# Expert outputs scattered by token on the way out, smaller tails, and half of the first attention's output projection moved forward

## The reference

```python
# layer 0 and 1 (first_block), ALPHA = 4 ** 0.25
h = layer_norm(ALPHA * h + mix, ln_g[i, 0], ln_b[i, 0])
ffn = hier_moe(h, ...)                    # 32 experts, D_EXPERT = 512, top 2 of one group of 8
h = layer_norm(ALPHA * h + ffn, ln_g[i, 1], ln_b[i, 1])
# layer 2 (second_block)
x = x + concat([att, lru_out]) @ w_out
y = hierarchical_moe(rmsnorm(x, ffn_norm), ...)    # 32 experts, D_EXPERT_2 = 256, top 2
return rmsnorm(x + y, final_norm)

# diff_attention, per head of 8 (two score maps m, head_dim 64, value width 128)
p = softmax(where(mask, s * scale, -inf))
a = p[:, :, 0] - lam * p[:, :, 1]
o = einsum('bhqk,bhkd->bhqd', a, v)
o = o * rsqrt(mean(square(o), -1) + 1e-5) * sub_g
return (o * (1 - lambda_init)) @ w_o
```

## Time and profile before

| | |
|---|---|
| median of 3 runs | 2256.73 us (2256.59 to 2259.34) |
| the profiled execution | 2260.55 us, of which the span is 2258.7 us |
| mean granted clock of TensorE | 0.947 of full speed |
| busy share of the span | PE 89%, PEld 48%, DVE 31%, ACT 15%, POOL 3% |
| moved by DMA | 624.71 MB, mean 277 GB/s |

### The profile page before, as it was taken

The page is one execution under the profiler, slowest core; times in us unless marked ns, Lnnn a source line. Parts: engine busy times, 40 slices in busy tenths (PEclk is TensorE's granted clock), DMA queues, the critical chain, the costliest instruction groups (busy, mean ns, idle before and its releaser), DMA issues.

```text
span 2258.7 us, 26007 instructions
## 1 busy us (share of the span) xinstructions
PE 2018.9 (89%) x9962; PEld 1091.9 (48%) x9962; DVE 696.9 (31%) x1601; ACT 339.4 (15%) x758; POOL 71.0 (3%) x97
## 2 busy tenths in 40 slices
PE   8999779999999995899999999995599899879772
PEld 4444446545554452756545554452564445544441
DVE  0166645211111112445211111112546225311114
ACT  1133321100000000111100000000133221111110
POOL 0000000000000001000000000001100001100001
PEclk9999879999999998899999999998798899889997
DMA  9911102999999998422999999999521011689995
GB/s 339 365 43 38 56 4 94 364 420 421 421 421 421 420 421 332 182 82 94 365 420 421 421 421 421 421 421 341 155 75 43 32 38 59 240 355 421 421 420 215
DMA packets 144273, 624.71 MB, mean 277 GB/s; under 512 B 13264, under 2 KB 52272, under 8 KB 82768
## 3 DMA queue, kind: packets, MB, share of 16 engines
q1 hardware_dynamic: 119344, 567.24, 62.7%
q0 software_dynamic: 9504, 31.42, 4.1%
q10 hardware_dynamic: 15360, 25.18, 3.0%
HBM read 574.50 MB, written 49.28 MB: 276 GB/s over the span
## 4 chain that ended last, share of the span: by engine, by line
PE 72%; DMA 16%; DVE 7%; ACT 2%; issue 2%; POOL 0%; SPq 0%; POOLq 0%; ACTq 0%; DVEq 0%
PE bank L762 16%; PE bank L789 9%; PE bank L747 9%; DMA ring<-in_moe_w_up_dram 8%; PE bank L539 7%; PE bank L648 6%; DMA ring<-in_w_up_dram 5%; PE bank L510 5%; PE bank L551 4%; PE bank L771 3%; PE bank L943 1%; DVE h L1190 1%; PE bank L904 1%; PE bank L738 1%; PE bank L604 1%
## 5 line engine op out<-in xcount | busy, mean ns | idle before, releaser
L762 PE MATMUL bank<-ring,work 128*64 128x512 f32 x2048 | 454.1, 593 | 5.3 <-DMA ring<-in_moe_w_up_dram 4.9
L1463 DVE TENSOR_TENSOR work<-work,bank 64x512 f32<-64x512 f32 (+1 forms) x96 | 87.1, 907 | 816.1 <-ACT work L1057 816.0
L789 PE MATMUL bank<-ring,work 128*64 128x512 f32 x1280 | 299.1, 605 | 3.6
L762 PEld LDWEIGHTS bank<-ring,work 128*64 128x64 f32 x2048 | 148.3, 137 | 299.1 <-issue 298.6
L747 PEld LDWEIGHTS bank<-work 128*128 128x128 f32 x2112 | 245.8, 191 | 57.3 <-issue 52.9
L747 PE MATMUL bank<-work 128*128 128x128 f32 x2112 | 271.1, 281 | 0.1
L539 PE MATMUL bank<-hT,ring 128*128 128x512 f32 x384 | 183.1, 614 | 0.7 <-ACT work L998 0.7
L789 PEld LDWEIGHTS bank<-ring,work 128*64 128x64 f32 x1280 | 83.7, 137 | 146.9 <-issue 129.6
L1061 ACT ACTIVATE work<-bank 128x512 f32<-128x512 f32 x96 | 57.4, 597 | 620.2 <-PE bank L789 610.8
L771 PE MATMUL bank<-ring,work 128*64 128x256 f32 x1024 | 117.0, 381 | 16.1 <-DMA ring<-in_w_up_dram 15.7
L1057 ACT ACTIVATE work<-bank 64x512 f32<-64x512 f32 (+1 forms) x96 | 49.8, 518 | 509.4 <-PE bank L762 399.9
(11 more groups left out here) (259 smaller groups left out, 1632.4 us busy)
## 6 DMA issues: line engine op xcount, KB each, us to landing
ring<-in_moe_w_gate_dram SPq DMA_DIRECT2D x128, 1024.0 KB, 17.3
ring<-in_moe_w_up_dram SPq DMA_DIRECT2D x128, 1024.0 KB, 19.2
ring<-in_moe_w_down_dram SPq DMA_DIRECT2D x128, 1024.0 KB, 17.3
ring<-in_w_gate_dram SPq DMA_DIRECT2D x32, 1024.0 KB, 20.8
ring<-in_w_up_dram SPq DMA_DIRECT2D x32, 1024.0 KB, 24.2
ring<-in_w_down_dram SPq DMA_DIRECT2D x32, 1024.0 KB, 23.1
y_rows<-work ACTq DMA_DIRECT2D x192, 128.0 KB, 6.8
x_rows<-zeros SPq DMA_DIRECT2D x1, 12800.0 KB, 54.3
```

What stands on the lines that cost most here:

```text
L762: mm = pe.matmul(GU[BLK * a:BLK * a + BLK, :], xT_[:, 4 * kk + k, :], v[:, k, :], start=(kk + k == 0), stop=(kk + k == 4))
L789: mm = pe.matmul(DN[BLK * n:BLK * n + BLK, :], hT_[:, 2 * kk + k, :], v[:, k, 512 * n:512 * n + 512], start=(kk + k == 0), stop=(2 * kk + ...
L1463: dve.tensor_tensor(dealt(hg[:, 0:F], F // P), as_dealt(sg[:, 0:F], F // P), as_dealt(GU[BLK:P, 0:F], F // P), ALU.mult).then_inc(b.hg, 1)
```

## The change

It has five parts.

1. **Expert outputs.** `ysb` now holds a pair of experts as 128 whole rows. POOL writes them with one indirect transfer per pair to `y_rows`, which has two rows per token; slots without a token have an index out of bounds and are left out. To know the token of each slot, POOL first scatters, with eight indirect transfers of 128 elements of 4 bytes, the row numbers (`token`) into `slot_token` in HBM and loads them back as a table of 32 by 64. PE turns the table ahead of expert 2 (in layer 2 ahead of expert 3), and DVE makes `y_row` of it.
2. **Tails.** SP loads each tile's rows with one plain transfer of 1 MB instead of POOL's two gathers. DVE's order is changed so that tile 0 is finished first; sums of squares move to ACT. `project_turned` goes tile by tile through the first two units (128 columns a matmul) and does the other two units with 512 columns at the end.
3. **First attention.** One `tensor_tensor_reduce` per map takes the place of mask, maximum and scaling. Heads 0 to 3 are normalized, turned and kept in steps 25 to 31; steps 32 to 39 multiply them with their half of the output weights (`project_heads`), DVE adds that into `h` (`add_heads`). After the attention only heads 4 to 7 are left.
4. **Row scatter of layer 2.** The indices for `x_rows` are worked out per tile (`rows_of`), and the transfers of a tile start when its own are known.
5. Semaphores are merged; rows for overflowing experts have a table of their own (`y_over`).

```diff
@@ PE, first attention
+            def project_heads(i):
+                tt, n = i // 2, i % 2
+                u = first["wo"] + 2 * n
+                if tt == 0:
+                    wait_unit(pe, u)
+                    pe.wait_ge(at.placed, 4)
+                    pe.wait_ge(at.rope, 15 + i)
+                else:
+                    pe.wait_ge(at.added, i - 1)
...
+                else:
+                    project_heads(st)
                 if pair >= 1:
                     scores(step - 8)
...
+                if 28 <= step < 32:
+                    turn_head(step - 28)
@@ PE, mixture
+                    if type(i) is int and s == (2 if l < 2 else 3):
+                        pe.wait_ge(slots_loaded, 16 * (l + 1))
+                        pe.transpose(CT[0:BLK, 192:192 + E], slot_tab, ident[0:E, 0:E]).then_inc(slots_turned, 1)
@@ ACT, mixture
-                    for n in range(2):
-                        act.dma_start(y_rows[bass.ts(block_row, BLK), 512 * n:512 * n + 512],
-                                      ysb[s][BLK * n:BLK * n + BLK, :]).then_inc(b.y_stored[s], 16)
+                    act.activation(ysb[s // 2][rows, 0:512], DN[0:BLK, :], ACT.Copy)
+                    act.activation(ysb[s // 2][rows, 512:D], DN[BLK:P, :], ACT.Copy).then_inc(b.ysb, 1)
@@ DVE, first attention, per map m
-                    link(dve.tensor_tensor(sc[:, P * qb:P * qb + P], sc[:, P * qb:P * qb + P], causal, ALU.add))
-                    link(dve.tensor_reduce(mx[:, m:m + 1], sc[:, 0:P * (qb + 1)], AX, ALU.max))
-                    dve.tensor_scalar(negmax[:, m:m + 1], mx[:, m:m + 1], -0.125, None, ALU.mult).then_inc(at.negmax, 1)
+                    dve.tensor_tensor_reduce(out=sc, in0=sc, in1=cmask[:, P * (3 - qb):4 * P], scale=1.0, scalar=3e38,
+                                             op0=ALU.add, op1=ALU.min,
+                                             accum_out=negmax[:, m:m + 1]).then_inc(at.negmax, 1)
...
+                if step >= 33:
+                    add_heads(step - 33)
@@ POOL, mixture
+                for tt in range(T):
+                    for k in range(2):
+                        pool.indirect_dma_start(
+                            out=slot_token[l], out_offset=bass.IndirectOffsetOnAxis(
+                                ap=idx[:, T * k + tt:T * k + tt + 1], axis=0),
+                            in_=token[:, T * k + tt:T * k + tt + 1], in_offset=None).then_inc(slots_dealt, 16)
...
+                pool.wait_ge(slots_known, l + 1)
+                for q in range(E // 2):
+                    if l == 2 and 4 <= q + 3 <= E // 2:
+                        load_rows(q + 3)
+                    pool.wait_ge(main.ysb, main.n0 + 2 * q + 2)
+                    pool.indirect_dma_start(
+                        out=y_rows, out_offset=bass.IndirectOffsetOnAxis(ap=y_row[:, q:q + 1], axis=0),
+                        in_=ysb[q % 2], in_offset=None, bounds_check=2 * S - 1, oob_is_err=False)\
+                        .then_inc(main.y_stored[q % 2], 16)
@@ SP, tail
+                sp.dma_start(ytile[tt], y_rows[2 * P * tt:2 * P * tt + 2 * P, :].rearrange("(p k) d -> p (k d)", k=2))\
+                    .then_inc(routing.gathered[tt], 16)
```

More of the change, by code:

```diff
@@ L340, in program @@
         ygat = [[wk(8192 + 2048 * i + 1024 * k, 1024) for k in range(2)] for i in range(T)]
+        ytile = [wk(8192 + 2048 * i, 2 * D) for i in range(T)]
         hn = wk(8192, 8192).rearrange("p (t d) -> p t d", t=T)[:, :, 0:D]
@@ L374, in program @@
         orstd = sm(452, 32).rearrange("p (t n) -> p t n", t=T)
-        rstd2 = sm(484, 4)
+        rstd2, eps6 = sm(484, 4), sm(488, 1)
+        token, later = sm(489, 8), sm(497, 1)
         ojunk = sb("ojunk", [P, P])[:, :]
@@ L496, in _ @@
             mixture(2)
+            sp.wait_ge(y_landed, 3)
+            for tt in range(T):
+                load_tile(tt)
             for tt in range(T):
@@ L505, in _ @@
         def _(pe):
-            def project_tokens(u, banks, half, th):
-                v = ring[u % UNITS][:, :].rearrange("p (k n) -> p k n", k=K)
-                for k in range(K):
-                    mm = pe.matmul(banks[:, 256 * th:256 * th + 256], v[:, k, 128 * half:128 * half + 128],
-                                   hT[:, k, 256 * th:256 * th + 256], start=(k == 0), stop=(k == K - 1))
-                if th == 1:
-                    mm.then_inc(units_used if half else half_unit, 1)
@@ L535, in project_t @@
+                for i in range(2, 4):
+                    wait_unit(pe, u0 + i)
+                    for half in range(2):
+                        project_t(u0 + i, bank[2 * i + half], half)
             def project_t(u, banks, half, ks=range(K)):
@@ L610, in permute, with turn_head @@
                 pe.matmul(bank[cc % 2][:, :], rope_p, raw[cc % 2], start=True, stop=True).then_inc(at.perm, 1)
+            def turn_head(hh):
+                pe.wait_ge(at.normal, hh + 1)
+                for tt in range(T):
+                    mm = pe.transpose(bank[6][:, P * tt:P * tt + P], o1[:, tt, P * hh:P * hh + P], ident)
+                mm.then_inc(at.turned, 1)
+            def project_heads(i):
[7 more added lines that the diff above has]
+                    pe.wait_ge(at.added, i - 1)
+                v = ring[u % UNITS][:, :].rearrange("p (k n) -> p k n", k=4)
+                for k in range(4):
+                    mm = pe.matmul(bank[n][:, :], o1[:, tt, P * k:P * k + P], v[:, k, :], start=(k == 0), stop=(k == 3))
+                mm.then_inc(at.part, 1)
             pe.wait_ge(at.v, 2 * T)
@@ L1231, in _ @@
             dve.memset(zeros[:, :], 0.0).then_inc(zero_ready, 1)
+            link(dve.memset(eps6, 1e-6))
+            dve.wait_ge(const_loaded, 16)
+            link(dve.tensor_reduce(later, tri, AX, ALU.add))
+            for tt in range(T):
+                for k in range(2):
+                    ins = dve.tensor_scalar(token[:, T * k + tt:T * k + tt + 1], later, -2.0,
+                                            float(2 * P * (tt + 1) + k - 1), ALU.mult, ALU.add)
+            link(ins)
             dve.wait_ge(par.lam, 64)
```

424 lines of the change are left out of this document (272 added, 152 removed).

## The result

The changed kernel takes 2207.68 us (median of 4 runs, 2203.96 to 2208.96) against 2256.66 us: a ratio of 0.978, 95% interval 0.9763 to 0.9797. Its profiled execution took 2207.31 us, of which the span is 2205.4. The forecast was 2202 us, range 2182 to 2226.

A forecast was written before the change was run, and what follows sets the result against it. PE and DMA both near their limit in the long mixtures, DMA in layer 2, a serial chain in the attention's last pair. Terms +8 - 3 - 9 - 3 - 17 - 25 - 5.5 = -54.5 gave 2206, by median 2202 us, range 2182 to 2226.

The forecast's parts named there:

- The sum of steps, 2206: Whole kernel: the stage terms add to -54.5 us against the profiled execution's 2260.55; chance 0.60, range 2194 to 2212.
- The 3.8 us that I took off for the median: Whole kernel: the old profiled execution was 3.8 us above the median, so 2206 became 2202 us.
- 67 us for eight steps: First attention, last pair: projection, scores, maxima, exponentials, combination and addition in series, 7.25 to 9.6 us per block.
- 9 for the clock: First attention and head: about half of eight projections at 1.2 GHz, 2 us lost each, and a cold head start: +9.
- the moved matmuls gain almost nothing (-1 us): First attention and head, clock aside: +2 + 26 - 5 - 23.7, as the new place isn't parallel to the chain.
- the shorter maximum gains nothing up to step 31: First attention up to step 31: PE is the bound, so the shorter mask and maximum gain nothing.
- Mixtures of layers 0 and 1: Fewer store bytes keep DMA from becoming the bound, -4.3 us; with 1 for small waits, -3 us each.
- Rival B: Skipped slots move bytes or cost descriptors: -15 in layer 2, nothing in the other mixtures, 2218 us; chance 0.12.
- rival C: Slot scatters do not overlap, table 120 us late in each of the first two mixtures: 2430 us; chance 0.05.
- if the DMA rate falls with the scattered writes: Sign, without a size, that the prediction is wrong.
- 8.5 + 36.8 + 3 + 27.5: Layer 0's tail: DVE's first tile, four PE tiles of 9.2, cold start, 64 instructions of 512 columns; 75.6 us against 82.2.
- the account of DMA time: Layer 2's mixture, DMA-bound: hole about 9 us, dealing 8, stores 10, less 2, so -25 us.

The follow-up runs named there:

- the trace with nothing dealt: Kernel before the change, with the eight transfers that deal layer 2's rows and the wait for them left out: 2241.75 us against 2256.53.
- seven like traces: Profiled executions of the changed kernel and six kernels made from it, all with the same first attention; step 32 begins at 257.5 to 261.1 us.
- the three kernels with 8.4, 4.2 and no MB: Changed kernel with empty slots written too, 2225.22 us; the changed kernel itself, 2207.68; changed kernel with every expert-output slot skipped, 2192.90.
- the other six traces: Profiled attention and tail experiments with layer 2's POOL queue and 4.2 MB of stores as in the changed kernel; layer 2 mixtures of 261.7 to 262.9 us.
- the two runs above: Changed kernel with layer 2's loads of pairs 2 and 3 ahead of the slot scatters, 2207.83 us; changed kernel without layer 2's slot scatters, 2206.16 us.
- the projection last: Changed kernel with the kept heads' projection moved to the end of its step, behind scores and values: 2175.41 us, ratio 0.9638 to before.
- the exponentials first: Kernel with the scores first, plus ACT's exponentials ahead of its copy of the group before in steps 32 to 39: 2174.61 us, ratio 0.9632 to before.
- the scores first: Changed kernel with the scores of a step computed ahead of the kept heads' projection in steps 32 to 39: 2188.62 us, ratio 0.9703 to before.

## Why the prediction was right, and where not

The time was 5.7 us above the forecast. The sum of steps, 2206, was right to 1.3 us against the profiled execution, because its two errors, +6 and +8, were met by 13 us more than forecast from tails, mixtures and the stages between. That they met is luck. The 3.8 us that I took off for the median had no counterpart: the profiled execution of the changed kernel is at its median.

**First attention: the mechanism was right, the price of the move was hidden in it.** The chain was worked out as 67 us for eight steps plus 9 for the clock; the eight took 337.85 - 261.05 = 76.8 us. The projections took 39.1 instead of 27.5, so the clock cost 11.6 where the forecast had 9, and five of eight projections were hit where it had half. Each of the five that took 5.3 to 6.5 us came after PE had stood 2.5 to 2.8 us for DVE's addition; the three of 3.7 us came after waits of at most 1.4 us. The other terms were each one or two us small: the stretch from the last step to the head 11.7 against 9.6, the head 61.1 against 59. Together 14 against 8. What failed is the sentence that the moved matmuls gain almost nothing (-1 us). As a sum for the whole of part 3, clock aside, it came near (14.1 - 11.6 = 2.5); but it credited the move with what the single reduction gives. Undone alone, the move costs 24 us. That the shorter maximum gains nothing up to step 31 is not refuted: with the reduction alone step 32 begins at 255.1, in the old first attention at 257.7 and, in the trace with nothing dealt, at 257.2, which is within the spread of seven like traces. The gain lies behind step 32.

**Mixtures of layers 0 and 1: right**, -3.6 and -4.3 against -3 each. Rival B (a skipped slot costs as much as a full one) is refuted by the three kernels with 8.4, 4.2 and no MB; rival C (scatters one behind another) by the windows, in which PE never waits. The sign "if the DMA rate falls with the scattered writes" did not come: with all rows scattered, 1960 to 2160 moved 421 GB/s, and before the change 2000 to 2200 moved 420. The rule of the Trainium skill that I weighed (DMA: Bandwidth & Descriptors, section Measured: under 64 KB the descriptors dominate) may hold for the transfers themselves. No run shows it in the time here, for taking eight scatters of 512 bytes away changed the median by 1.5 us, within its spread.

**Tails: the mechanism was right, with one link overlooked in layer 0 and too much caution in layer 1.** In layer 0 the first tile lands 11.0 us after the last matmul (forecast 13.5, before 15.5):

```profile
895.91 4.89 DMA work<-y_rows
900.83 1.29 DVE h L1267
...
913.49 9.67 PE bank L548 x64
...
924.28 7.41 PE bank L548 x64
```

That is the chain of the changed kernel in tail 0; a tile costs PE 7.41 + 0.45 + 0.61 us and the waits between, 8.54, where I had 9.2; the first one took 9.67, a cold start of 2.3 (forecast 3). PE begins to turn tile 0 at 909.42, 8.6 us after the landing, as forecast (8.5); but it begins to project 12.7 us after it, where turn and copy should have taken 1.6 more. ACT's queue explains the rest:

```profile
912.61 0.20 ACT L1051 ACTIVATE small<-small 128x1 f32<-128x1 f32 x1 [7.05 <-DVE small L1281]
912.84 1.08 ACT L1041 ACTIVATE hT<-bank 128x512 f32<-128x512 f32 x2
```

The copies of the turned tile 0 (L1041) stand behind the square root of tile 1 (L1051), which waits for DVE's variance of tile 1. It is the link of the first attention again, worth some 2.5 us here; no run opened it. The sum itself, 8.5 + 36.8 + 3 + 27.5, is 75.8 and not 75.6; measured were 75.4. In layer 1 the landing takes 11.5 us, PE's work then goes as forecast but for a cold start of 1.0 us instead of 3.

**Layer 2: the step that failed is the account of DMA time**, "the hole of about 9 us, some 8 us of dealing, 4.2 MB of stores = 10 us, less 2". The mixture took 264.3 us, where "near 255" was to be seen. The windows give its bytes: 108.4 MB before, 102.0 after, and 102.0 to 102.2 in the other six traces. The 6.3 MB are 15 us at 420 GB/s: 4.2 MB of stores, 10 us as forecast, and only 2.1 MB of dealing, 5 us and not 8. Of the eight dealing transfers the last four start on POOL from 1908.67 to 1912.50, about when expert 0 does (1910.5), so their rows still land in the mixture. What is left of the 15.7 to 18.3 us that the mixture lost is 1 to 3 us for the hole, where the forecast had 9 - 2 = 7. With nothing dealt it was 4. So the dealing was 3 us too dear and the hole 4 to 6; together they are the 8 us. This is an account from rates and not an experiment: these 2.1 MB of dealing fall in the first microseconds, when no weight load is due before 1914.90, and whether they cost their 5 us wasn't tried. The slot scatters and the wait of 4.28 us are out as causes, by the two runs above.

**Last tail**: -5.9 against -5.5.

## What to carry to other kernels

Before work is moved from a busy stage into the gaps of another, follow the in-order queue of every engine round one step: if the moved piece stands ahead of anything that the next link of the chain needs, also through another engine's queue, it lengthens the chain by its own time. Here the same move of eight projections cost 24 us with them at the head of their steps and gained 7 (by the medians) with them at the end.

When several edits share a stage, undo each alone: one of two that the stage's time had netted was worth some 10 us, the other cost 24. And in an account of DMA time, check with a window how many bytes fall within the stage: of 4.2 MB that were to leave it, half stayed. A wait seen in one trace is worth a look at the same stretch in a second: the one of 4.28 us was in one of seven.

The best version found puts the projection last or the exponentials first: 2174.6 to 2175.4 us, 3.6 to 3.7% below the kernel before the change, 1.5% below the change itself.

## What the runs showed of the hardware

- An indirect transfer whose indices are out of bounds takes POOL as long as any other (a mean of 979 to 982 ns with no, half and all of its rows skipped). Skipping 1024 rows of 4 KB took 7.1 and 9.8 us off a mixture that is bound by DMA.
- Eight indirect transfers of 128 elements of 4 bytes start 1.27 us apart on POOL (1918.21 to 1927.05), and the last had landed by 1933.7, some 6.6 us after its start. The forecast took 5 us for it.
- PE's granted clock was 0.87 over eight steps in which five of eight projections (3.44 us of work at full clock) came after waits of 2.5 to 2.8 us and then took 5.3 to 6.5; it was 1.00 over the same instructions with waits of at most 0.7 us. With the scores first, four projections came after waits of 1.6 us: three of them took 3.70 us and one 5.26.
